# A two-layer encoder step: two full tiles and nine seven-product pairs at the start of each feed-forward stage, with more of the low parts split by VectorE

## The reference

```python
def swiglu(h, w_in, w_out):
    gate, up = split_cols(h @ w_in, (D_FF, D_FF))      # D_FF = 2816, h: 576 x 1024
    return (jax.nn.silu(gate) * up) @ w_out

for i in range(DEPTH):                                 # DEPTH = 2
    ...                                                # mixer, residual
    h = ada_modulate(rms_norm(x, g_ffn[i]), sh2, sc2)
    x = x + gt2[:, None, :] * swiglu(h, w_ffn_in[i], w_ffn_out[i])
```

## Time and profile before

| | us |
|---|---|
| median of 3 runs | 1533.57 (1532.62 to 1533.80) |
| the profiled execution | 1533.63 |
| its span, first to last instruction | 1531.5 |
| TensorE busy | 1492.0 (97%) |
| VectorE busy | 1069.4 (70%) |
| ScalarE busy | 634.3 (41%) |
| GpSimd busy | 580.4 (38%) |

### The profile page before, as it was taken

The page is one execution under the profiler, slowest core; times in us unless marked ns, Lnnn a source line. Parts: engine busy times, 40 slices in busy tenths (PEclk is TensorE's granted clock), DMA queues, the critical chain, the costliest instruction groups (busy, mean ns, idle before and its releaser), DMA issues.

```text
span 1531.5 us, 29136 instructions
## 1 busy us (share of the span) xinstructions
PE 1492.0 (97%) x11405; PEld 1373.2 (90%) x11405; DVE 1069.4 (70%) x2057; ACT 634.3 (41%) x1265; POOL 580.4 (38%) x346
## 2 busy tenths in 40 slices
PE   5999999999999999999999999999999999999998
PEld 2768956899999999999888888887999999999998
DVE  1659888668887778876644444457988877688753
ACT  3434366344552145522533333334254541355423
POOL 1234841225771066722322222231227640376421
PEclk8999999999999999999999999999999999999999
DMA  9874510341344433452254444443532355333521
GB/s 335 269 264 150 141 39 2 96 114 40 104 128 159 148 83 89 116 173 67 77 167 127 127 127 127 127 128 100 171 91 56 93 168 167 86 108 83 156 79 62
DMA packets 244454, 189.21 MB, mean 124 GB/s; under 512 B 12888, under 2 KB 228608, under 8 KB 240112
## 3 DMA queue, kind: packets, MB, share of 16 engines
q1 hardware_dynamic: 231232, 178.61, 38.9%
q10 hardware_dynamic: 13104, 8.97, 1.9%
HBM read 175.44 MB, written 8.50 MB: 120 GB/s over the span
## 4 chain that ended last, share of the span: by engine, by line
PE 86%; DVE 7%; ACT 3%; issue 2%; DMA 1%; POOL 0%; ACTq 0%; SPq 0%; POOLq 0%; DVEq 0%
PE lin L860 40%; PE lin L1440 28%; PE lin L877 5%; PE S L1201 2%; PE O L995 1%; PE O L1331 1%; PE O L1254 1%; DVE acc_out L2666 1%; PE T L1234 1%; PE S L1064 1%; DMA ada_raw<-in_w_ada 1%; PE S L1120 1%; ACT act_hi L1665 1%; PE lin L1300 1%; PE T L1291 0%
## 5 line engine op out<-in xcount | busy, mean ns | idle before, releaser
L2147 POOL TENSOR_TENSOR w_lo<-w_raw,w_hi 128x1024 fp32r<-128x1024 f32 (+3 forms) x68 | 168.3, 2476 | 409.6 <-ACT w_hi L1612 409.6
L2238 POOL TENSOR_TENSOR w_lo<-ada_raw,w_hi 128x512 fp32r<-128x512 f32 x114 | 156.9, 1378 | 241.8 <-ACT w_hi L1913 241.8
L1612 ACT ACTIVATE w_hi<-w_raw 128x1024 fp32r<-128x1024 f32 (+2 forms) x110 | 125.2, 1139 | 224.7 <-PE lin L860 212.3
L860 PE MATMUL lin<-act_hi,w_hi 128*128 128x288 f32 (+1 forms) x1088 | 164.6, 302 | 5.3 <-ACT act_hi L1644 2.0
L860 PE MATMUL lin<-act_hi,w_lo 128*128 128x288 f32 (+1 forms) x1088 | 167.3, 299 | 0.2
L860 PEld LDWEIGHTS lin<-act_hi,w_hi 128*128 128x128 f32 (+1 forms) x1088 | 149.5, 189 | 15.5 <-issue 10.1
L860 PE MATMUL lin<-act_lo,w_hi 128*128 128x288 f32 (+1 forms) x1088 | 162.1, 298 | 0.0
L860 PEld LDWEIGHTS lin<-act_hi,w_lo 128*128 128x128 f32 (+1 forms) x1088 | 149.9, 188 | 7.5 <-issue 6.7
L860 PEld LDWEIGHTS lin<-act_lo,w_hi 128*128 128x128 f32 (+1 forms) x1088 | 149.6, 188 | 3.4 <-issue 2.9
L2238 POOL TENSOR_TENSOR w_lo<-s_tmp,w_hi 128x512 fp32r<-128x512 f32 x76 | 129.2, 1717 | 15.0 <-ACT w_hi L1916 15.0
L1440 PE MATMUL lin<-act_hi,w_hi 128*128 128x288 f32 x608 | 105.4, 295 | 0.0
(11 more groups left out here) (347 smaller groups left out, 3031.1 us busy)
## 6 DMA issues: line engine op xcount, KB each, us to landing
ada_raw<-in_w_ffn_in SPq DMA_DIRECT2D x76, 512.0 KB, 5.2
w_raw<-in_w_ffn_out SPq DMA_DIRECT2D x32, 704.0 KB, 4.9
ada_raw<-in_w_ada SPq DMA_DIRECT2D x20, 1024.0 KB, 7.6
ada_raw<-in_w_ada SPq DMA_DIRECT2D x32, 512.0 KB, 5.0
w_raw<-in_w_in_b SPq DMA_DIRECT2D x32, 512.0 KB, 4.2
w_raw<-in_w_in_a SPq DMA_DIRECT2D x16, 512.0 KB, 6.2
ada_qo<-in_w_ada SPq DMA_DIRECT2D x8, 1024.0 KB, 7.5
ada_raw<-in_w_ada_final SPq DMA_DIRECT2D x16, 512.0 KB, 5.6
```

Of the source, the lines that this page charges most:

```text
L860: last = nc.tensor.matmul(lin_u(u)[0:m, tok], w, (lo if p == 2 else hi)[:, at(t) if at else t, tok], start=(p == 0 and t == 0), stop=(p == ...
L1612: A(w_hi[:, u % 2, 0:n], w_raw[:, u % 2, 0:n], ACT.Copy).then_inc(whi_done, 1)
L2147: TT(w_lo[:, u % 2, 0:n], w_raw[:, u % 2, 0:n], w_hi[:, u % 2, 0:n].bitcast(F32), ALU.subtract)\
L2238: TT(ring(w_lo, q), raw, ring(w_hi, q).bitcast(F32), ALU.subtract).then_inc(ws_lo_p, 1)
```

## The change

`FULL` goes from 3 to 2, so each layer has two full tiles and nine pairs in its first half. The units after it are renumbered, with the same parity as before. VectorE now makes the low parts of the weights of units 2 and 3 (the second full tile), and `T_lo[0]`, `[1]` and `[2]`; GpSimd makes no `T_lo`, and `A11`'s low part of the first pair stands ahead of the others. The third difference, `t_part` 2, and S4's weight sum move behind the last full tile's gate product. The steps at which the ring skips a slot are two instead of four.

```diff
-FULL = 3
+FULL = 2
...
-OUT_UNITS = [u0 + m for u0 in (U_OA, U_OB, *U_OUT) for m in range(1, KT)]
+OUT_UNITS = [U_F0 + 2, U_F0 + 3, U_F1 + 2, U_F1 + 3] + [u0 + m for u0 in (U_OA, U_OB, *U_OUT) for m in range(1, KT)]
...
-            at += n in ((2, 3, 5, 6), (2, 4, 6))[h % 2]
+            at += n in ((3, 6), (2, 4, 6))[h % 2]
...
                 if fresh and i in (W_S1, W_S2, W_S3, W_A22):
-                    pe.wait_ge(th_done, 4 * layer + {W_S1: 1, W_S3: 2, W_S2: 3, W_A22: 4}[i])
+                    pe.wait_ge(th_done, 4 * layer + {W_S1: 1, W_S2: 2, W_S3: 3, W_A22: 4}[i])
...
-                        if i in (W_S1, W_S2):
-                            pe.wait_ge(tl_p, 2 * layer + (1 if i == W_S1 else 2))
-                        if i in (W_S3, W_A22):
-                            pe.wait_ge(tl_v, 2 * layer + (1 if i == W_S3 else 2))
+                        if i in (W_S1, W_S2, W_S3, W_A22):
+                            pe.wait_ge(tl_v, 4 * layer + {W_S1: 1, W_S2: 2, W_S3: 3, W_A22: 4}[i])
...
@@ ScalarE
-                for j in (0, 2, 1):
-                    t_hi(layer, j)
-                in_tile(u0, base, 1, lambda: split_hi(u0 + 4, N))
-                split_hi(u0 + 5, N)
+                t_hi(layer, 0)
+                t_hi(layer, 1)
...
-                in_tile(u0, base, 2, first_parts)
-                hi_part(n0, W_S2)
+                    hi_part(n0, W_S2)
+
+                in_tile(u0, base, 1, first_parts)
                 hi_part(n0, W_S3)
+                t_hi(layer, 2)
                 pair_stage(n0, n0 + N_A, U_OUT[2 * layer])
...
@@ GpSimd
-                for i in (W_A11, W_S2, W_S3):
+                for i in (W_S2, W_S3):
                     lo_part(n0, i)
...
-                for u in range(u0 + 1, u0 + 2 * FULL):
-                    split_lo(u, N)
-                for j in range(2):
-                    t_lo(layer, j)
+                split_lo(u0 + 1, N)
+                lo_part(n0, W_A11)
                 pair_stage(n0, n0 + N_A, U_OUT[2 * layer])
                 out_stage(U_OUT[2 * layer], 0)
+                lo_part(n0 + N_A, W_A11)
...
@@ VectorE
                 t_part(layer, nz, 0)
                 full_gate(0, NB)
-                t_part(layer, nz, 2)
+                split_lo(u0 + 2, KT * P)
+                t_part(layer, nz, 1)
                 full_lo(0)
-                t_part(layer, nz, 1)
+                t_lo(layer, 0)
+                split_lo(u0 + 3, KT * P)
                 t_part(layer, nz, 3)
-                t_lo(layer, 2)
-                full_gate(1)
-                full_lo(1)
+                t_lo(layer, 1)
                 if layer == 1:
                     sum_mods(5)
                 first_sums(n0)
-                full_gate(2)
-                full_lo(2)
+                full_gate(1)
+                t_part(layer, nz, 2)
+                s_add(n0, W_S4)
+                t_lo(layer, 2)
+                full_lo(1)
                 pair_stage(n0, n0 + N_A)
```

More of the change, by code:

```diff
@@ L495, in encoder_step @@
             sem("sp_done"), sem("x1_done"), sem("sv_step"), sem("sg_done"), sem("hf_done"))
-        t_raw, th_done, tl_p, tl_v = sem("t_raw"), sem("th_done"), sem("tl_p"), sem("tl_v")
+        t_raw, th_done, tl_v = sem("t_raw"), sem("th_done"), sem("tl_v")
         y_free, y_scaled, y_shifted = sem("y_free"), sem("y_scaled"), sem("y_shifted")
@@ L1939, in t_hi @@
             def t_hi(layer, j):
-                act.wait_ge(t_raw, 4 * layer + {0: 1, 2: 2, 1: 3, 3: 4}[j])
+                act.wait_ge(t_raw, 4 * layer + {0: 1, 1: 2, 3: 3, 2: 4}[j])
                 if j < 3:
@@ L2750, in t_part @@
                 if j == 3:
-                    dve.wait_ge(t_raw, t0 + 3)
+                    dve.wait_ge(t_raw, t0 + 2)
                 for t in range(4):
@@ L2766, in t_lo @@
             def t_lo(layer, j):
-                if j == 2:
-                    dve.wait_ge(th_done, 4 * layer + 2)
-                    V.tensor_tensor(T_lo[:, 2, :, :], T_raw[:, 2, :, :], T_hi[:, 2, :, :].bitcast(F32),
+                dve.wait_ge(th_done, 4 * layer + j + 1)
+                if j < 2:
+                    dve.wait_ge(t_raw, 4 * layer + j + 2)
+                if j < 3:
+                    V.tensor_tensor(T_lo[:, j, :, :], T_raw[:, j, :, :], T_hi[:, j, :, :].bitcast(F32),
                                     ALU.subtract).then_inc(tl_v, 1)
                 else:
-                    dve.wait_ge(th_done, 4 * layer + 4)
                     V.tensor_tensor(act_lo[:, 0:4, HALF:TOK], T4_raw[:, :, :], act_hi[:, 0:4, HALF:TOK].bitcast(F32),
@@ L2888, in first_sums @@
                     dve.wait_ge(t_free, T_ADA3 if n < N_A else T_H[(0, 5, 6)[half_of(n) - 1]] + 1)
-                    for i in (W_S1, W_S2, W_S3, W_S4):
+                    for i in (W_S1, W_S2, W_S3):
                         s_add(n, i)
+                    if n in FIRST[1:4:2]:
+                        s_add(n, W_S4)
                     lo_part(n, W_S1)
```

## The result

The changed kernel takes 1539.53 us (median of 5 runs, 1537.38 to 1541.37) against 1532.84 (1532.62 to 1533.80) in runs of the kernel before beside it: a ratio of 1.0042 (95% interval 1.0031 to 1.0053). A second series gave 1539.14 us (1538.24 to 1539.44) against 1532.80 (27 runs, 1531.39 to 1535.20), a ratio of 1.0041 (1.0028 to 1.0055). The forecast was 1540.1 and slower. The execution whose profile is read first took 1538.67 us, span 1536.9.

A forecast was written before the change was run, and what follows sets the result against it. TensorE's matmul count was taken as the bound, unless other engines make it wait. Two layers of 5.3 us waits less 4.1 saved gave +6.5 us on 1533.63: 1540.1 us, range 1534 to 1546.

The forecast's parts named there:

- What it saves: TensorE matmuls and waits no longer needed with one full tile fewer per layer: 4.1 us in all.
- `t_part` 2 held twice: First pair, VectorE: GpSimd's S2 and S3 low parts hold its first two instructions; the third difference is complete at 370.1.
- the walk: Step-by-step timing of the engines through layer 0's first pair: 5.3 us of waits per layer.
- Wait before S3: First pair: TensorE waits 1.9 us for T_hi of the third difference, and 0.1 more for starting again.
- `full_lo` held by A12's low part: First pair, VectorE: it stands still until GpSimd's instruction ends at 373.85, taking 1.9 us instead of 0.76.
- the sum behind it: VectorE's next weight sum, held by GpSimd's A22 low part until 375.75: 1.8 us.
- Wait before S4: First pair: TensorE waits 2.2 us for VectorE's U1, and 0.1 more.
- The sum: Whole kernel: two layers losing 5.3 us each, less 4.1 saved, is +6.5 us: 1540.1 us, +0.42%.
- A first pair of 16.4 us: Sign in the trace: each layer's first pair takes some 16.4 us, the other pairs 11.14.
- C: Rival, 16%: TensorE's clock falls around the first pair's two idle times, at most 3.4 us per fall: 1541 to 1547 us.
- A: Main case, 50%: the step-by-step timing holds, 1540.1 us, within 1537 to 1543.
- Rival D: 12%: VectorE's short `t_part` 2 instructions get in ahead of GpSimd, the difference is in time, 1529.5 us.

The follow-up runs named there:

- the second profile: The changed kernel as it is, run and profiled again beside the later orders: 1539.14 us, ratio 1.0041 to the kernel before.
- the matmuls put in: Changed kernel with 13 throwaway matmuls on TensorE while it waits for T_hi of the third difference, in each layer's first pair: 1538.89 us, ratio 1.0040.
- the order alone: Changed kernel, only VectorE's first-pair order rewritten: half of the third difference before the third weight sum, U1 before the full tile's low part: 1532.31 us, ratio 0.9999.
- the three new orders: Changed kernel with VectorE's first-pair order rewritten: U1 earlier (1535.27 us); also half the third difference earlier (1532.31); also two low parts moved to VectorE (1528.65).
- the last version: Changed kernel with VectorE's first-pair order rewritten and low parts of the second and third weight sums moved from GpSimd to VectorE: 1528.65 us, ratio 0.9976.
- U1 first: Changed kernel, but in each layer's first pair VectorE makes U1 right behind the full tile's low part, ahead of the next weight sums: 1535.27 us, ratio 1.0016.

## Why the prediction was right, point by point

1. **What it saves.** From unit 2 to the first pair of layer 0: 12.91 us in the second profile (351.61 to 364.52), against 26.05; 13.14 less, which is the 12.80 of a tile and 0.34 where 0.3 was put. In layer 1 the same stretch went from 26.09 to 13.28, 12.81 less: the 0.1 allowed there was nothing.
2. **`t_part` 2 held twice.** 1.59 us for the first instruction, as in the walk (1.6). Wait before S3 forecast 1.9, measured 1.79 in each profile of the changed kernel.
3. **`full_lo` held by A12's low part.** This was the step that no row before showed and that the Trainium skill's rule (page "SBUF — State Buffer", section "Who interferes with whom") decided: a VectorE instruction with two SBUF inputs contends with a GpSimd instruction that reads SBUF. The trace agrees: 1.85 us with the low part beside it, 0.75 with it left out. Forecast 1.9; the sum behind it 1.8, measured 1.76. The kernel before held a control that the prediction did not use: the pairs' low part of a gated tile (L2835) is the same operation at the same size, with its first operand in PSUM. At 405.16 it took 0.76 us beside a GpSimd instruction that ran from 404.67 to 405.96, and all 38 of them took 0.76. So it is the place of the operand and not the operation that decides here.
4. **Wait before S4.** Forecast 2.2, measured 2.02 at full clock, 0.85 where the clock fell ahead of it. A reader of the first profile alone would have put this step down as half wrong; the second shows that the wait was there, filled with slow passes.
5. **The sum.** A first pair of 16.4 us at full clock was forecast, 16.39 is measured in the one first pair of the changed order at full clock (layer 1 with the matmuls put in): 5.25 us over 11.14 instead of 5.3. The terms fit one by one there. S3 starts 1.88 us late, S4 another 2.2, A22 another 0.53. Without the clock the two layers give 2 x (16.39 - 11.32) + 2 x 11.14 - 13.14 - 12.81 = 6.5 us, the forecast's 6.5.
6. **The clock.** It was priced as a rival (C, 16%), but it happened beside A: falls of 3.4 us in the first pairs of both profiles, costing 0 and 0.9 us a layer. This the sum left out. Against it, the fall of 6.8 us in the norm stretch of layer 1 was 3.4 us long in the first profile and absent in the second, where the way from the first pair of layer 0's second half to unit 2 of layer 1 is 1.59 us shorter than in the kernel before (541.67 to 1137.10, against 537.83 to 1134.85). In the second profile 1.8 us lost and 1.6 gained nearly cancel. A third term nobody had in the sum: at the output matrix behind the first half of layer 1 TensorE waited for the last pair's low part, before (first row) for 0.63 us, in the changed kernel for 0.26:

```profile
1253.67 0.54 PE L860 MATMUL lin<-hid_hi,w_hi 128*128 128x288 f32 x2 [0.63 <-DVE hid_lo L2835]
```

```profile
1259.82 0.54 PE L860 MATMUL lin<-hid_hi,w_hi 128*128 128x288 f32 x2 [0.26 <-DVE hid_lo L2825]
```

With it, and with the 0.15 us by which unit 2 of layer 0 came earlier, 6.5 + 1.8 - 1.6 - 0.4 - 0.15 gives 6.15, and the span is 6.1 us longer than the kernel before's (1537.6 against 1531.5). The forecast of 6.5 had none of these last four terms; that they nearly cancel is luck, and the total fits better than the list of its causes.

Rival D fell: the short instructions did not get in ahead. A third difference that is in time came only with GpSimd's two low parts left out or given to VectorE.

## What to carry to other kernels

Where VectorE and GpSimd both read two SBUF operands, plan them as one resource at the start of a stage: here a low part of 1.30 us on GpSimd cost VectorE more standing still than the 0.68 us of making it itself, so two of them given to the busier engine, with the order fitted to it, shortened the total by 3.7 us more than the order alone. Taking out a tile that covered the preparation of the next stage saves its matmuls only if each operand of the next products is ready one tile earlier; walk the other engines through that stretch first, and put what frees a bank ahead of what can be held. And compare waits of two profiles only after you have looked at the granted clock between them, since slow passes fill a later wait (2.02 us shrank to 0.85 here).

## What the runs showed of the hardware

- The mutual hold is regular enough to plan with: the first pairs that the expectations of the three new orders give (14.6, 13.3, and 11.2 to 11.6 us), from a replay of the trace's durations, were measured at 14.48, 13.31 and 11.66 us in layer 0, and at 14.96 (with a fall of the clock), 13.14 and 11.49 in layer 1.
- Runs of one kernel differ by 1 to 5 us, whatever the kernel: the kernel before by 1.2, 3.1 and 3.8 us in its three series (5, 21 and 27 runs), the changed kernel by 4.0 and 1.2 (5 each), the last version by 5.1 (11). Falls of the clock are a part of that. The profiled execution of the last version lies 3.2 us over its median and reached unit 2 at 354.99; the order-only version, profiled at 1531.90, reached it at 351.57. Some 1.7 of these 3.4 us arise in the fall of 6.8 us at 338.59, which the other did not have. The rest was there already before 203 us, with no fall behind 46 us: the execution with U1 first had no fall in the norm stretch of layer 0 either and reached unit 2 at 353.71. What makes this second part was not looked into, and no run here kept the clock up in the norm stretch.
- A12's low part on GpSimd took 1.94 us instead of 1.30 while VectorE's `T_lo[2]` was running: the hold goes both ways.
